# The three mixers of a two-block network: pieces of both attentions woven between the halves of later weight units, masked quarters and unused halves left out

## The reference, cut to what matters

```python
    proj = x @ w_in
    fq, fk, fv, ff, dq, dk, dv, hq, hf, hi, hg = _split_columns(proj)
    log_f = jax.nn.log_sigmoid(ff.astype(jnp.float32) + fox_fb.astype(jnp.float32))
...
        logits = jnp.einsum('bhqd,bhkd->bhqk', q_blk, k).astype(jnp.float32) * scale
        logits = logits + c_blk[..., :, None] - cum[..., None, :]
        logits = jnp.where(key_pos[None, :] <= q_pos[:, None], logits, -jnp.inf)
...
        p = attn_map(q1b, k1) - lam * attn_map(q2b, k2)
...
    y = jnp.concatenate([_merge_heads(y_fox).astype(x.dtype), _merge_heads(y_diff).astype(x.dtype),
                         _merge_heads(y_hgrn).astype(x.dtype)], axis=-1)
    return y @ w_out
```

## Time and profile before

| | |
|---|---|
| median of 3 runs | 2556.11 us (2554.0 to 2558.41) |
| the profiled execution | 2555.8 us |
| its span, first to last instruction | 2554.0 us |
| mean granted clock of PE | 0.943 of full speed |
| PE busy | 2305.1 us (90%) |
| DVE busy | 1718.6 us (67%) |
| ACT busy | 1336.2 us (52%) |
| mean DMA rate | 234 GB/s |

### The profile page before, as it was taken

How to read it: one execution, slowest core, us unless ns; L and a number is a source line. 1 busy time by engine, 2 the same in 40 slices (tenths; PEclk the granted TensorE clock), 3 DMA queues, 4 the chain that set the end, 5 groups by cost and what they waited for, 6 DMA issues and landing times.

```text
span 2554.0 us, 30321 instructions
## 1 busy us (share of the span) xinstructions
PE 2305.1 (90%) x11625; PEld 1930.3 (76%) x11625; DVE 1718.6 (67%) x1542; ACT 1336.2 (52%) x1166; POOL 26.4 (1%) x50
## 2 busy tenths in 40 slices
PE   6988999897869999999999999997876899599996
PEld 6757998864768888888888888886855768588885
DVE  4225454593538898989898989897445714488886
ACT  4024333424327777777777777775433213267774
POOL 2000000000000000000000000000000000000000
PEclk9999999998979999999999999998885999599998
DMA  7243455430239999999999999996430232399993
GB/s 264 100 172 116 149 198 178 152 132 30 78 128 348 342 366 337 357 347 355 343 364 340 357 346 362 332 370 244 137 105 30 83 136 68 126 344 332 333 330 124
DMA packets 269353, 597.13 MB, mean 234 GB/s; under 512 B 9008, under 2 KB 33792, under 8 KB 269280
## 3 DMA queue, kind: packets, MB, share of 16 engines
q1 hardware_dynamic: 264944, 582.01, 63.8%
q0 software_dynamic: 4336, 14.10, 1.6%
HBM read 595.02 MB, written 1.05 MB: 233 GB/s over the span
## 4 chain that ended last, share of the span: by engine, by line
PE 78%; DVE 6%; ACT 4%; issue 2%; ACTq 0%; POOL 0%; DVEq 0%
PE ps L643 21%; PE ps L645 20%; PE ps L644 20%; PE ps L586 3%; PE ps L873 2%; PE ps L581 2%; PE ps L906 1%; DVE w_low L1875 1%; PE ps L822 1%; PE ps L849 1%; PE ps L630 1%; ACT w_high L1358 1%; PE ps L891 1%; PE ps L677 1%; ACT L1358 1%
## 5 line engine op out<-in xcount | busy, mean ns | idle before, releaser
L1875 DVE TENSOR_TENSOR w_low<-ring,w_high 128x2048 fp32r<-128x2048 f32 x432 | 983.6, 2289 | 137.5 <-ACT w_high L1358 136.7
L1358 ACT ACTIVATE w_high<-ring 128x2048 fp32r<-128x2048 f32 x432 | 822.7, 1915 | 180.7 <-PE ps L645 180.6
L644 PE MATMUL ps<-w_high,parts 128*128 128x512 f32 (+1 forms) x2024 | 790.4, 391 | 0.0
L643 PE MATMUL ps<-w_high,parts 128*128 128x512 f32 x1816 | 720.5, 397 | 30.5 <-DVE w_low L1875 26.8
L645 PE MATMUL ps<-w_low,parts 128*128 128x512 f32 x1816 | 710.8, 391 | 0.0
L644 PEld LDWEIGHTS ps<-w_high,parts 128*128 128x128 f32 x2024 | 384.6, 190 | 75.1
L643 PEld LDWEIGHTS ps<-w_high,parts 128*128 128x128 f32 x1816 | 342.9, 189 | 107.5 <-issue 35.5
L645 PEld LDWEIGHTS ps<-w_low,parts 128*128 128x128 f32 x1816 | 342.6, 189 | 73.0
L1501 DVE TENSOR_TENSOR w_low<-ring,w_high 128x2048 fp32r<-128x2048 f32 (+2 forms) x93 | 206.8, 2244 | 132.9 <-ACT w_high L1153 132.2
L1153 ACT ACTIVATE w_high<-ring 128x2048 fp32r<-128x2048 f32 (+2 forms) x93 | 173.0, 1873 | 184.1 <-PE ps L645 144.0
L643 PE MATMUL ps<-XT_high,w_high 128*128 128x256 f32 x896 | 258.5, 288 | 10.0 <-DVE parts L1490 6.2
(11 more groups left out here) (344 smaller groups left out, 1955.2 us busy)
## 6 DMA issues: line engine op xcount, KB each, us to landing
ring<-in_od_moe_gu SPq DMA_DIRECT2D x224, 1024.0 KB, 7.2
ring<-in_od_moe_down SPq DMA_DIRECT2D x112, 1024.0 KB, 6.9
ring<-in_w SPq DMA_DIRECT2D x96, 1024.0 KB, 7.2
ring<-in_ev_ffn_gu SPq DMA_DIRECT2D x22, 1024.0 KB, 7.4
ring<-in_xa_wkv SPq DMA_DIRECT2D x8, 2048.0 KB, 8.1
ring<-in_od_pw_w SPq DMA_DIRECT2D x6, 2048.0 KB, 8.6
ring<-in_w_in SPq DMA_DIRECT2D x6, 2048.0 KB, 7.9
ring<-in_ev_ffn_down SPq DMA_DIRECT2D x11, 1024.0 KB, 5.1
```

The lines of the kernel that those rows point to most:

```text
L643: mm(out_, xh, wh, start=start, stop=False)
L644: mm(out_, xl, wh, start=False, stop=False)
L1358: A(w_high[:, j % SPLITS, :], ring[:, j % NS, :], ACT.Copy).then_inc(moe_sem(k, "high"), 1)
L1875: V.tensor_tensor(w_low[:, j % SPLITS, :], ring[:, j % NS, :], w_high[:, j % SPLITS, :].bitcast(F32), SUB)\
```

## The change

- The units come in the order fqk, fv, hf, dqk, dv, hq, hi, hg.
- The pieces of both attentions, the transposed keys, the diagonal and the first spans stand on PE between the halves of later units. Their scores use banks 4 to 7, while the units keep banks 0 to 3.
- For the first 128 queries only the first 128 keys are scored, masked, exponentiated, divided, transposed and multiplied (the other quarter of each map is masked in both attentions).
- The forget gate's part for the keys is added to the scores by PE itself, as further products with the negated gate in the same accumulation (L977 and L981 to L983 of the changed kernel); the eight additions for the bias on DVE fall away, the sum of the query goes in with the mask.
- In the level loop DVE multiplies only the late half of the queries and the early half of the keys, PE's scores are 64 columns wide, and the merge takes those columns.
- ACT and DVE split three halves of out0 and out1 behind levels 2, 4 and 6; the variance of the difference heads' norm comes behind level 3, its scaling behind the loop, ACT's silu of hg behind its last exponential.
- POOL loads the level constants once the first mixture is done, ahead of the mask row.
- Three pairs of semaphores are merged (`exp_wanted`, `log1p_ready`, `conformer_by_...`).

The units:

```diff
-_unit("dqk", "w_in_2", 772, 512, True, "x")
-_unit("hq", "w_in_2", 1540, 512, True, "x")
 _unit("fv", "w_in_2", 512, 260, False, "x")
-_unit("dv", "w_in_2", 1284, 256, False, "x")
 _unit("hf", "w_in_2", 2052, 512, False, "x")
+_unit("dqk", "w_in_2", 772, 512, True, "x")
+_unit("dv", "w_in_2", 1284, 256, False, "x")
+_unit("hq", "w_in_2", 1540, 512, True, "x")
```

The late half of each block of a level, for every head and token block (`early` is the same with 0:m):

```diff
+        def late(t, lv):
+            m = 1 << lv if lv < 7 else P
+            return t.rearrange("p h t -> p (h t)").rearrange("p (b n) -> p b n", n=2 * m)[:, :, m:2 * m]
```

The loads of POOL:

```diff
-            pool.wait_ge(S("fox_scored"), 1)
+            pool.wait_ge(S("moe_done"), 1)
             pool.dma_start(ring[:, 6, 0:a - RESIDENT], const_in[:, RESIDENT:a])\
                 .then_inc(S("levels_loaded"), 16)
+            row(0, const_in[:, a:a + D])
```

The list of PE up to the level loop:

```diff
+            project("fqk", first=True)
+            project("fv")
+            project("hf", halves=(0,))
+            fox_sums()
+            pe.wait_ge(S("fox_sums_read"), 1)
+            fox_scores()
+            project("hf", halves=(1,))
+            project("dqk", halves=(0,))
+            turn_map(1)
+            project("dqk", halves=(1,))
+            attend_map(1, FV)
+            turn_keys()
+            project("dv")
+            evicted("dqk")
+            pe.wait_ge(S("keys_columns"), 1)
+            pe.wait_ge(S("small_read"), 1)
+            diff_scores(0)
+            project("hq", halves=(0,))
+            pe.wait_ge(S("diff_map"), 1)
+            diff_scores(1)
+            project("hq", halves=(1,))
+            project("hi", halves=(0,))
+            pe.wait_ge(S("diff_map"), 2)
+            diagonals()
+            project("hi", halves=(1,))
+            pe.wait_ge(S("level_merged"), 1)
+            turn_map(2)
+            project("hg", halves=(0,))
+            evicted("dv")
+            attend_map(2, DV)
+            evicted("hf")
+            pe.wait_ge(S("levels_loaded"), 16)
             level_spans(0)
+            project("hg", halves=(1,))
+            pe.wait_ge(S("small_read"), 2)
             level_spans(1)
+            evicted("hi")
```

The level loop of DVE:

```diff
-                V.tensor_tensor(QE, QH, E, MUL)
-                V.tensor_tensor(KE, KH, E, MUL).then_inc(S("level_decayed"), 1)
+                V.tensor_tensor(late(QE, lv), late(QH, lv), late(E, lv), MUL)
+                V.tensor_tensor(early(KE, lv), early(KH, lv), early(E, lv), MUL).then_inc(S("level_decayed"), 1)
...
+                merge(lv)
+                if lv == 3:
+                    head_variance(h4(OD), h4(XS[:, :, 512:768]), 64)
+                if lv in (2, 4, 6):
+                    lows(halves_to("out0", -2 + lv // 2))
+            head_scale(h4(OD), 64, dgain, 1.0 - LAM_INIT)
```

More of the change, by code:

```diff
@@ L964, in _ @@
[L964 to L970, removed]
@@ L1022, in _ @@
[L1022 to L1031 removed]
+                    last.then_inc(S("diff_scores"), 1)
@@ new lines, in turn_map @@
+            def turn_map(n):
+                first, second = MAPS[n]
+                pe.wait_ge(S("probs_ready"), 2 * n)
+                for place in range(4):
+                    o = ps[:, 4 + place // 2, place % 2 * T:place % 2 * T + T]
+                    nc.tensor.transpose(o[:, 0:P], first[:, place, :], IDENT)
+                    nc.tensor.transpose(o[:, P:T], second[:, place, 0:P], IDENT)
+                    last = nc.tensor.transpose(ps[:, 6, place * P:(place + 1) * P], second[:, place, P:T], IDENT)
+                last.then_inc(S("probs_turned"), 1)
@@ new lines, in attend_map @@
+            def attend_map(n, v):
+                first, second = MAPS_T[n]
+                pe.wait_ge(S("probsT_by_act"), n)
+                pe.wait_ge(S("probsT_by_vector"), n)
+                for place, h in enumerate(HEAD_ORDER):
+                    d = slice(h * 64, (h + 1) * 64)
+                    mm(ps[:, 7, d], first[:, place, 0:P], v[:, 0, d], start=True, stop=True)
+                    o = ps[:, 7, T + h * 64:T + (h + 1) * 64]
+                    mm(o, first[:, place, P:T], v[:, 0, d], start=True, stop=False)
+                    last = mm(o, second[:, place, :], v[:, 1, d], start=False, stop=True)
+                last.then_inc(S("small_attended"), 1)
@@ new lines, in _ @@
+            A(LF, LF, ACT.Ln, bias=1.0).then_inc(S("log1p_ready"), 1)
+            A(KR, PAIRS[u % 2], ACT.Sigmoid, scale=-1.0).then_inc(S("recurrent_keys"), 1)
+            map_columns(1)
+            highs(halves_to("dv"))
+            take_columns("dqk", DQK)
+            highs(halves_to("hq", -1))
+            act.wait_ge(S("keys_turned"), 1)
+            A(KH, ps[:, 4:6, :].rearrange("p a (b t) -> p (a b) t", t=T), ACT.Copy).then_inc(S("keys_columns"), 1)
+            act.wait_ge(S("keys_columns"), 1)
@@ new lines, in _ @@
+            masks = row(0).rearrange("p (k a t) -> p k a t", k=2, a=2)
+            for tc in range(2):
+                dve.wait_ge(S("fox_scores"), tc + 1)
+                for place, h in enumerate(HEAD_ORDER):
+                    last = V.scalar_tensor_tensor(MAPS[1][tc][:, place, :], map_scores(tc)[:, place // 2, place % 2, :], cs[:, tc, h:h + 1],
+                                                  masks[:, 0, tc, 0:(tc + 1) * P], ADD, ADD)
+                step(last)
+            map_max(1)
@@ new lines, in _ @@
+            step(masked_map(0))
+            dve.sem_inc(S("diff_map"), 1)
+            map_max(2)
+            lows(halves_to("hi", -1))
+            step(normalise_map(2))
+            use_row(0, masked_map(1))
+            dve.sem_inc(S("diff_map"), 1)
+            map_max(3)
+            lows(halves_to("hi"))
+            step(normalise_map(3))
+            first, second = w_(8192, 12 * P), w_(9728, 12 * P)
+            V.scalar_tensor_tensor(first, second, nlam[:, 0:1], first, MUL, ADD).then_inc(S("probs_ready"), 2)
```

468 lines of the change are left out of this document (220 added, 248 removed).

## The result

The changed kernel takes **2492.07 us** (median of 4 runs, 2491.16 to 2493.01) against 2556.45 before (4 runs): ratio 0.9749, 95% interval 0.9732 to 0.9766. That is 64.4 us less; forecast were 73, in a range that holds the result. The profiled execution took 2491.16 us, its span 2489.4 at a mean clock of 0.952.

What follows compares the result with a forecast made beforehand. The attentions were taken as bound by a chain of PE, DVE and ACT taking turns. 1900.9 + 25.9 + 2.0 + 2.3 + 3.0 + 8.4 = 1942.5 against 2017.2, with 1.7 taken back: -73, so 2483 us, range 2470 to 2502.

Steps and rivals of the forecast that it cites:

- late handoffs: Rival: PE waits at eight woven pieces for a split, 2.3 us and 1.7 of half clock each: 2515 us, chance 0.14.
- Item 1: Attention pieces, turned keys, diagonals and first spans move between projection halves on PE, keeping their own PE time: 24.8 us.
- The low end for narrow partitions: 256-wide score rows with 64 or 32 partitions might take 0.12 us each instead of 0.22: 2.7 us less.
- Item 2: Projections no longer wait: 13.6 us of waits go, 1.7 come, weights and probabilities otherwise 3 us ahead; hg ends at 1900.9.
- Item 3: Level loop with halved DVE operands: PE is the bound, 64-column scores gain nothing; 25.9 us after hg, waits 2.0 and 2.3.
- Item 4: Behind the level loop nothing is removed: recurrence and its drain 3.0 us, DVE's chain 8.4.
- one stretch of half clock: Allowance for PE running at half clock behind a wait, once: 1.7 us, turning -74.7 into -73.
- Item 5: Loads: level constants issued earlier by GpSimd, weight panels ahead of use; the norm might wait up to 4 us, taken as 0.
- Item 6: Masked quarters left out and forgetting bias inside the scores shorten DVE's work under PE's cover: nothing beyond item 1.
- DVE's halves without worth: Rival: halving DVE's operands in the level loop saves nothing, +7 us: 2490 us, chance 0.06.
- table loads: Rival: each of ACT's eight table switches holds it 1.28 us longer, all on the chain, 10 us: 2493 us, chance 0.03.
- The clock stays low: Rival: narrow pieces hold PE's clock down across the projections too, up to 132 us more: 2615 us, chance 0.03.

Runs made afterwards that it cites:

- before_halves: The kernel before with only DVE's products of the level loop halved: 2553.02 us.
- two_ahead: The changed kernel with forgetting scores regrouped by weight height, gate's sums in bank 2 with their wait later, out0 split ahead of the loop, out1 behind merge 1: 2476.25 us.
- more_maxima: The changed kernel with each of the six row maxima of the masked maps taken three times on DVE: 2503.66 us.
- same_rows: The changed kernel with the forgetting scores' q times k over all 128 feature partitions instead of 64, so all weights there have one height: 2483.41 us.
- regroup: The changed kernel with the forgetting scores reordered, 3 changes between 64-row and 128-row weights instead of 15, nothing left out: 2483.00 us.

## Why the prediction was right or wrong

The direction, the size and the mechanism (PE's queue filled, attentions under the projections) were right; the kernel is 9.1 us slower than forecast. From H to XS the forecast was 152.9 and 161.6 came. That the result lies in the range is in part luck: its upper end, 2502, was drawn for late handoffs, which did not come, and what came in their place was priced nowhere.

- **Item 1 is the step that failed**, in one term: the forgetting scores, "5.4 (a further 0.8 for the switch of shapes, an allowance)". They took 16.2. The allowance covers less than a quarter of what the order costs: 15 changes of weight height instead of 3 cost 3.6 us at full clock, and with the clock down 7.1 more came. The sum priced each row by its columns at full clock and took no account of what stood beside it; and the clock was taken as back for good behind dense passes, while it fell at 1.24 us of wait. The low end for narrow partitions was right for the difference scores: 1.68 us each, 3.4 for the two instead of 5.3.
- **Item 2**: right but for one handoff. Waits of 1.24 us instead of 1.7, none for splits; the clock is 0.99 behind the scores. hg ended at 1909.5 instead of 1900.9: 10.0 from the scores, less 1.9 and 0.5, and 1.0 of small terms (0.6 of it the first passes behind the scores at half clock). But "some 3 us or more ahead" was wrong at the diagonals, where the margin is 0.14: the averages of DVE's and ACT's work over 106 us hid a stretch of 27 us in which DVE never rests.
- **Item 3**: 30.4 us from hg to the recurrence for 30.2. PE is the bound up to the last levels, and the scores of 64 columns gain nothing: a level takes 3.57 us with them and also in before_halves, where they have 128. The Trainium skill's table (TensorE: Matmul & The Clock Gate, Back-to-back issue gap) has some 60 cycles for up to 64 columns against 134 for 128; by that ratio 6.9 us of the 12.5 would have gone (an estimate from the page; the prediction's 6.3 is a plain half), and none of it came. The same section says that in a stream of weight loads and products both set the spacing, and this the trace bears out: 16 loads take 1.87 us, as long as their 16 products (rows below). The halves of DVE take 0.69, as taken, and are worth 3 to 6. Of the merges two take 1.31 and not 0.7, which costs nothing here, since DVE waits for PE in those levels. Level 1 in the changed kernel's timeline:

```profile
1916.62 1.87 PEld L1056 LDWEIGHTS ps<-work 128*128 128x128 f32 x16
1916.72 1.90 PE L1056 MATMUL ps<-work 128*128 128x64 f32 x16
```

- **Item 4**: DVE's chain 8.5 for 8.4, but the recurrence with its drain 4.7 for 3.0, at half clock behind the 2.1 of wait. That is where the 1.7 for one stretch of half clock went, but it was not the only one: besides the scores of item 1, the last eight score rows took 1.67 us behind a wait of 1.27, for 1.16 at full clock in two_ahead.
- **Item 5**: right, nothing.
- **Item 6**: its sum holds, its reason only in part. In the kernel before the masked quarters are worth 4.2 us in the attentions for three maps, and more_maxima shows that what DVE does more at the difference maps shows in full. So at these two maps their omission, some 1.4 us a map, is probably part of what lets the weave close; no run put the quarters, or the bias on DVE, back into the changed kernel.
- **Rivals.** Late handoffs, DVE's halves without worth and table loads (eight up to the end of hg, two behind it, 1.28 each, the next activation 0.02 behind where its input is there) did not come. "The clock stays low" did, in small: not through the narrow pieces as a kind, since turned maps, attended products and spans ran at full clock, but through the one group of them that alternates.

## What to carry to other kernels

Put float32 products whose weights differ in height (64 and 128 partitions) into groups of one height where the accumulation allows it, and look at the start-to-start time of the rows, not at busy time: PE read as 100% busy in the stretch that lost 10 us. A wait of one or two microseconds ahead of such a group or of a short last stage mostly cost the clock as well in these traces, so move the work that stands in the way into a place where the queue is idle by the trace; two_ahead gained three times its wait. Check the cover place by place, by the gap between the last producer and its consumer, since an engine busy for less than 60% of the stretch can have no margin at one handoff.

## What was not expected of the hardware

- In strict alternation a pair of rows with 64-partition weights behind one with 128, or the reverse, starts 0.42 us behind it at full clock and 0.72 at half, where pairs of one height take 0.23 and 0.43; the 32-partition scores among themselves, 16 rows in 1.68, show nothing of it. The Trainium skill (TensorE: Matmul & The Clock Gate, Step-by-step: what each phase is for) says that weight loads are pulled ahead of running matmuls if the row groups don't conflict or the load goes to the background buffer, and that for the time of a load the row count doesn't matter. The idle 0.22 us ahead of each alternated load fits a load that isn't pulled ahead. The second half of the rule holds for the load itself, 0.50 us for a pair of either height there, but the count does matter where it changes. That conflicting row groups are the cause is not shown, and it can't be the whole reason: weights of 128 partitions behind others of 128 would conflict as well and show no such stall.
- PE at 100% busy for 16.2 us at half clock, with alternation (five traces), and back at full clock after 3.4 us without it (one trace, same_rows). Dense passes behind the alternation needed 1.0 us in one execution of the changed kernel and 4.4 in the other. Behind waits of 1.23 to 1.25 us the clock fell in six traces and not in that of regroup; what decides it stays open.
- DVE's copy_predicated of 512 elements takes 1.31 us with masks of runs of 1 and 2 elements and 0.72 from runs of 4 on; of 1024 elements without strides 1.33.
